# Reading q by feature, and a new order at the heads of the delta tiles, in a hybrid decoder layer on one core

## The reference: one layer of a hybrid decoder

```python
    qb = _l2norm(heads(qb, DK)) * (DK ** -0.5)      # x * rsqrt(sum(x * x) + eps)
    kb = _l2norm(heads(kb, DK))
...
def _gated_delta_chunk(S, q, k, v, g, beta):
    gc = jnp.cumsum(g, axis=-1)
    diff = gc[..., :, None] - gc[..., None, :]
    decay = jnp.where(incl, jnp.exp(jnp.where(incl, diff, 0.0)), 0.0)
    kk = jnp.einsum('bhid,bhjd->bhij', k, k)
    a_mat = jnp.where(strict, beta[..., :, None] * decay * kk, 0.0) + jnp.eye(L, dtype=jnp.float32)
    eg = jnp.exp(gc)
    rhs = beta[..., None] * (v - eg[..., None] * jnp.einsum('bhid,bhde->bhie', k, S))
    u = lax.linalg.triangular_solve(a_mat, rhs, left_side=True, lower=True, unit_diagonal=True)
    qk = jnp.einsum('bhid,bhjd->bhij', q, k) * decay
    o = eg[..., None] * jnp.einsum('bhid,bhde->bhie', q, S) + jnp.einsum('bhij,bhje->bhie', qk, u)
    S_new = jnp.exp(gc[..., -1])[..., None, None] * S + jnp.einsum('bhjd,bhj,bhje->bhde', k, w_last, u)
    return S_new, o
...
ob = _gated_rms_norm(ob, z, gdn_norm)               # o * rsqrt(mean(o * o) + eps) * w * silu(z)
gate = sigmoid(gate_logits); h = h + (ga * (oa @ w_oa) + gb * (ob @ w_ob)) @ w_out
```

## Time and profile before

| | us |
|---|---|
| median of three runs (lowest, highest) | 3335.37 (3330.85, 3346.25) |
| the profiled execution's own time | 3332.55 |
| its span | 3330.7 |
| TensorE busy, share of the span | 3247.1 (97%) |
| weight loads on TensorE, which overlap its products | 2841.8 (85%) |
| VectorE, ScalarE, GpSimd busy | 60%, 46%, 12% |

### The profile page before, as it was taken

One profiled execution on the slowest core, in us unless ns is written; L12 is line 12 of the kernel. 1 busy time (PEld: TensorE's weight loads), 2 busy tenths in 40 slices (PEclk: granted clock), 3 DMA queues, 4 the chain that ended last, 5 costly groups with the idle time before them and its releaser, 6 DMA issues. The chain is left out here.

```text
span 3330.7 us, 59185 instructions
## 1 busy us (share of the span) xinstructions
PE 3247.1 (97%) x23574; PEld 2841.8 (85%) x23574; DVE 1986.5 (60%) x3721; ACT 1520.0 (46%) x3173; POOL 413.5 (12%) x453
## 2 busy tenths in 40 slices
PE   8999899999999999999999999999999999999998
PEld 7877789999998777898998777889998777789896
DVE  6645545543547654685766754587575855578484
ACT  5324443222235554464554654455454654446362
POOL 2211100432503111000003011000001211000000
PEclk9989999999999999999999999999999999999999
DMA  4211013655743111354553211345463211246463
GB/s 161 63 56 46 25 58 111 229 194 199 257 154 110 54 46 63 116 160 138 165 193 109 73 39 46 114 137 167 137 213 124 78 44 43 80 129 183 124 177 97
DMA packets 142816, 392.47 MB, mean 118 GB/s; under 512 B 18288, under 2 KB 20288, under 8 KB 139072
## 3 DMA queue, kind: packets, MB, share of 16 engines
q1 hardware_dynamic: 142544, 388.69, 36.5%
HBM read 353.95 MB, written 35.69 MB: 117 GB/s over the span
## 5 line engine op out<-in xcount | busy, mean ns | idle before, releaser
L624 DVE TENSOR_TENSOR wl<-raw,wh 128x512 fp32r<-128x512 f32 (+1 forms) x795 | 747.1, 947 | 573.2 <-ACT wh L617 569.6
L617 ACT CAST wh<-raw 128x512 fp32r<-128x512 f32 (+1 forms) x795 | 636.0, 808 | 459.6 <-PE bank L892 370.8
L892 PE MATMUL bank<-xnT,wh 128*128 128x512 f32 (+2 forms) x2432 | 725.3, 382 | 9.0 <-ACT gate L1663 7.3
L892 PE MATMUL bank<-hnT,wh 128*128 128x256 f32 (+2 forms) x3016 | 580.7, 290 | 3.1 <-ACT V L1959 3.1
L892 PEld LDWEIGHTS bank<-xnT,wh 128*128 128x128 f32 x2432 | 430.3, 192 | 81.6 <-issue 16.5
L892 PEld LDWEIGHTS bank<-hnT,wh 128*128 128x128 f32 x3016 | 473.6, 188 | 8.5 <-ACT V L1959 3.7
L892 PE MATMUL bank<-hid,wh 128*128 128x512 f32 (+1 forms) x1760 | 467.6, 353 | 0.0
L892 PE MATMUL bank<-xnT,wl 128*128 128x512 f32 (+2 forms) x1280 | 461.8, 365 | 0.0
L892 PE MATMUL bank<-hnT,wl 128*128 128x256 f32 (+2 forms) x1508 | 437.2, 290 | 0.0
L892 PE MATMUL bank<-Tm,wh 128*128 128x256 f32 x2016 | 368.7, 282 | 0.2 <-ACT sg L1959 0.2
L892 PEld LDWEIGHTS bank<-hid,wh 128*128 128x128 f32 x1760 | 309.5, 188 | 46.0 <-issue 0.3
(11 more groups left out here) (380 smaller groups left out, 4527.3 us busy)
## 6 DMA issues: line engine op xcount, KB each, us to landing
raw<-in_wstream SPq DMA_DIRECT2D x346, 512.0 KB, 3.5
raw<-wsum SPq DMA_DIRECT2D x252, 256.0 KB, 3.4
raw<-in_wstream SPq DMA_DIRECT2D x189, 256.0 KB, 2.8
ops_in<-in_wstream SPq DMA_DIRECT2D x44, 512.0 KB, 7.6
wsum<-ops_out SPq DMA_DIRECT2D x22, 1024.0 KB, 6.3
hT<-in_xT SPq DMA_DIRECT2D x4, 2048.0 KB, 8.9
out_yp_out<-hT SPq DMA_DIRECT2D x16, 512.0 KB, 3.0
xr<-in_x_prompt SPq DMA_DIRECT2D x12, 512.0 KB, 7.9
```

The costliest lines, as they stand in the source:

```text
L617: act.copy(hi_cell(n), raw_cell(n)).then_inc(sem("hi_done"), 1)
L624: nc.vector.tensor_tensor(lo_cell(n), raw_cell(n), hi_cell(n).bitcast(F32), ALU.subtract).then_inc(sem("lo_done"), 1)
L892: ins = nc.tensor.matmul(*a, **k)
```

## The change

- The product of k and q (kq) reads q by feature straight from `post`, not normalised. Its norm factor is put on the output instead: GpSimd multiplies the sum of the output's squares by the square of the factor, and the root that it makes of it by the factor.
- `d_qn` and `d_qe` go, with their two transposes back and ScalarE's two copies of them. In their place ScalarE exponentiates the decay that TensorE has spread over a bank (`eG`, 128x512), and VectorE multiplies `post` by it (`scaled_q`, into `d_WQ`). The transpose of q to rows stays for tiles 1 to 3, whose sums of squares need it, and goes for the small tile and tile 0.
- VectorE at a tile's head: the arguments come right behind `d_kn`, the sum of q's squares (now three reductions, with the halves of two heads swapped) behind them; the weights' subtraction and `delta_out` come behind the masks, the scaled rows and `scaled_q`.
- ScalarE: the copy of the gate logits comes ahead of the cast of the next unit, which came first before. A unit that is done at k = 17 is cast at the next tile's head, behind the decays.
- Group 0's tables: in the small tile the state products go by head, with three quarters between them; tiles 0 to 2 get a quarter at k = 17; the last tile has seven in place of eleven. Of the small tile's own loop over the eight sequences (`S_FILL`) a quarter moves from b = 0 to b = 5.

```diff
-QUARTERS_S = (1, 1, 1, 1, 1, 1, 0, 0, 1, 0, 0, 0, 0, 1, 2, 6, 0, 0)
-QUARTERS_0 = (1, 1, 1, 0, 1, 1, 1, 1, 0, 1, 1, 0, 1, 0, 1, 0, 0, 0)
-S_FILL = (0, 3, 4, 6, 7, 8)
-assert sum(QUARTERS) * NT == 64 and QUARTERS_C + sum(QUARTERS_S) + sum(QUARTERS_0) * NT == 64
+QUARTERS_S = (1, 1, 1, 1, 1, 1, 0, 0, 1, 0, 0, 0, 0, 1, 3, 6, 0, 0)
+QUARTERS_0 = (1, 1, 1, 0, 1, 1, 1, 1, 0, 1, 1, 0, 1, 0, 1, 0, 0, 1)
+QUARTERS_E = (1, 0, 1, 0, 1, 0, 1, 0, 0, 1, 0, 0, 1, 0, 1, 0, 0, 0)
+S_FILL = (3, 4, 5, 6, 7, 8)
+assert sum(QUARTERS) * NT == 64 and QUARTERS_C + sum(QUARTERS_S) + sum(QUARTERS_0) * (NT - 1) + sum(QUARTERS_E) == 64
...
-        quarters_of = lambda t: QUARTERS_S if t == "S" else QUARTERS_0 if first else QUARTERS
+        quarters_of = lambda t: QUARTERS if not first else QUARTERS_S if t == "S" else QUARTERS_E if t == NT - 1 else QUARTERS_0
...
+                if q_rows(t):
+                    rows_from(t, 2, 0, "sqc_done", 2 * NH + 2 * t)
...
-                pe.wait_ge(*made("bt_rd", 3 * i + 2))
                 claim(2, "QK_done", i + 1)
                 for x in range(NH):
                     for cs in chunks(t):
-                        last = nc.tensor.matmul(bank[2][cs, w * x:w * (x + 1)], kTd[:, x, cs], qT[:, x, cs], start=True, stop=True)
+                        last = nc.tensor.matmul(bank[2][cs, w * x:w * (x + 1)], kTd[:, x, cs], q_of(x, cs), start=True, stop=True)
...
 
                 if first or t:
-                    turned(t, 0, 1, "kn")
-                    turned(t, 1, 3, "qn")
+                    turned(t)
                 beside(t, 0)
                 if first or t:
                     delta_scores(t)
-                if first or t:
-                    turned(t, 2, 5, "qe")
                     beside(t, 1)
...
                     for x in range(NH):
+                        if x:
+                            gate_quarter()
                         pair = WQ[:, x, 0:2 * CH].rearrange("p (s c) -> p s c", c=CH)
                         out = bank[3][:, 2 * CH * x:2 * CH * (x + 1)].rearrange("p (s c) -> p s c", c=CH)
                         for b in range(NB):
                             own = slice(NMETA + NL * b, NMETA + NL * (b + 1))
                             last = nc.tensor.matmul(out[:, :, own], Sb[:, b, x, :], pair[:, :, own], start=True, stop=True)
-                        if x == 1:
-                            gate_quarter()
                     last.then_inc(sem("WS_ps"), 1)
-                    gate_quarter()
...
-                hi_until("gate", j)
...
+                act.activation(eG[:, :, 0:n], bank[4][:, 0:NH * n].rearrange("p (h n) -> p h n", h=NH), ACT.Exp).then_inc(sem("dec_done"), 1)
...
                     if quarters[0] % 4 == 0:
                         gate_logits()
+                        if k != 17:
+                            gate_weights()
...
                 if first or t:
-                    turned_copy(t, 0, 1, "kTd")
-                    turned_copy(t, 1, 3, "qT")
-                    delta_decays(t)
+                    turned_copy(t)
+                    if t != 0:
+                        delta_decays(t)
+                    gate_weights()
                 beside(t, 0)
-                turned_copy(t, 2, 5, "qeT")
...
-                root(rr[0:n, 8:12], ss[0:n, 8:12], n, 1.0 / P, 4).then_inc(sem("orr_done"), 1)
+                own = lambda x: fac[0:n, slot(t), x, :]
+                link(nc.gpsimd.tensor_tensor(ss[0:n, 12:16], ss[0:n, 8:12], own(1), ALU.mult))
+                link(root(rr[0:n, 8:12], ss[0:n, 12:16], n, 1.0 / P, 4))
+                nc.gpsimd.tensor_tensor(rr[0:n, 8:12], rr[0:n, 8:12], own(0), ALU.mult).then_inc(sem("orr_done"), 1)
...
+            def scaled_q(t):
+
+                n = n_of(t)
+                dve.wait_ge(*made("dec_done", 10 * ix[t] + 6))
+                v_.tensor_tensor(WQ[:, :, CH:CH + n], post[:, 0:NH, col(t):col(t) + n], eG[:, :, 0:n], ALU.mult).then_inc(sem("natq_done"), 1)
+
+            def sum_k(t):
+
+                dve.wait_ge(*made("sqc_done", 2 * NH + 2 * t - 1))
+                v_.tensor_reduce(out=rs8[:, t + 1, NH:], in_=q4["kn"][:], op=ALU.add, axis=AX.X).then_inc(sem("sums_in"), 1)
+
+            def sum_q(t):
+
+                dve.wait_ge(*made("sqc_done", 2 * NH + 2 * t))
+                step(v_.tensor_reduce(out=rs8[:, t + 1, 0:2], in_=q4["qn"][:, 0:2], op=ALU.add, axis=AX.X))
+                for dst, src in HALVES:
+                    ins = v_.tensor_reduce(out=rs8[dst, t + 1, 2:NH], in_=q4["qn"][src, 2:], op=ALU.add, axis=AX.X)
+                    if dst.start == 0:
+                        step(ins)
...
-                if t == "S" or t and not first:
+                if t == "S":
                     delta_args(t)
-                if i:
-                    delta_out(tiles[i - 1])
                 beside(t, 0)
                 if first or t:
                     delta_masks(t)
-                    dve.wait_ge(*made("nat_ps", 3 * i + 3))
+                    dve.wait_ge(*made("nat_ps", nat_of(t, 2 + q_rows(t))))
+                    if q_rows(t):
+                        dve.wait_ge(*made("rs_done", 1 + F + 2 * t))
                     scaled(t, ("kb", "kw", "bv"))
+                    scaled_q(t)
+                    gate_weights()
                 else:
                     scaled(t, ("kb", "kw"))
                 beside(t, 1)
+                if i:
+                    delta_out(tiles[i - 1])
...
-                            row_sums_of(t + 1)
+                            sum_k(t + 1)
...
                             delta_rows(t + 1)
-                        if first and k == 1 and t + 1 < NT:
                             delta_args(t + 1)
+                            sum_q(t + 1)
                         beside(t, 15 + 2 * k)
```

More of the change, by code:

```diff
@@ L179 @@
         (0, 15, 12):
-            "bt_ps bt_rd nat_ps",
+            "",
         (0, 16, 0):
@@ L784, in group @@
         chunk_half = lambda x, k: k if x < NH // 2 else 1 - k
-        quarters_of = lambda t: QUARTERS_S if t == "S" else QUARTERS_0 if first else QUARTERS
+        quarters_of = lambda t: QUARTERS if not first else QUARTERS_S if t == "S" else QUARTERS_E if t == NT - 1 else QUARTERS_0
+        q_rows = lambda t: t not in ("S", 0)
+        nat_of = lambda t, k: sum(2 + q_rows(x) for x in tiles[:ix[t]]) + k
         def sync(sp):
@@ L1170, in delta_rows, with turned @@
                 last.then_inc(sem("G_ps"), 1)
-            def turned(t, q, b, src):
+            def turned(t):
                 i, n = ix[t], n_of(t)
-                pe.wait_ge(*made("natq_done", 6 * i + q + 1))
-                claim(b, "bt_rd", 3 * i + q + 1)
+                pe.wait_ge(*made("natq_done", 5 * i + 1))
+                claim(1, "bt_rd", i + 1)
                 for x in range(NH):
-                    last = nc.tensor.transpose(bank[b][:, n * x:n * (x + 1)], q4[src][0:n, x, :], c("ident")[0:n, 0:n])
+                    last = nc.tensor.transpose(bank[1][:, n * x:n * (x + 1)], q4["kn"][0:n, x, :], c("ident")[0:n, 0:n])
                 last.then_inc(sem("bt_ps"), 1)
@@ L1789, in scalar @@
                 gate_logits()
+                hi_until("gate", 0)
             def beside(t, k):
@@ L2367, in sums_copied @@
                 for n, sl in heads_of:
[L2368 removed]
+                    sums = bank[6][0:n, 8 * sl.start:8 * sl.stop].rearrange("p (t h) -> p t h", h=8)
+                    if n == P:
+                        step(v_.tensor_copy(rs8[:, sl, 0:2], sums[:, :, 0:2]))
+                        for dst, src in HALVES:
+                            step(v_.tensor_copy(rs8[dst, sl, 2:NH], sums[src, :, 2:NH]))
+                        v_.tensor_copy(rs8[:, sl, NH:], sums[:, :, NH:]).then_inc(sem("sums_in"), 1)
+                    else:
+                        v_.tensor_copy(rs8[0:n, sl, :], sums).then_inc(sem("sums_in"), 1)
+                settle()
             for j in range(NCONV):
@@ L2444, in beside @@
                     quarters[0] += 1
-                    if quarters[0] % 4 == 0:
-                        lo_until("gate", quarters[0] // 4 - 1)
+                    if quarters[0] % 4 == 0 and k != 17:
+                        gate_weights()
                     if first and quarters[0] % 4 == 2:
@@ L2450, in beside, with gate_weights @@
                     attention_step(after(t), IN_DELTA_S if t == "S" else IN_DELTA, k)
+            def gate_weights():
+                if quarters[0] >= 4:
+                    lo_until("gate", quarters[0] // 4 - 1)
             def delta_out(t):
```

99 lines of the change are left out of this document (51 added, 48 removed).

## The result

| | before | changed |
|---|---|---|
| median of 8 runs (lowest, highest), us | 3340.86 (3330.85, 3348.92) | 3354.72 (3349.59, 3357.66) |
| the profiled execution's own time | 3332.55 | 3352.43 |

The ratio is 1.0042, with a 95% interval of 1.0026 to 1.0058. The forecast was 3320, in a range of 3305 to 3335.

What follows compares the result with a forecast made beforehand. TensorE, busy for 97% of the span, was taken as the bound. Groups 1 to 3 (-2.2) and group 0 (-11.4) made -13.6, from 3332.55 to 3319 us; the forecast was 3320, range 3305 to 3335.

Steps and rivals of the forecast that it cites:

- Group 0: First group's tiles: transposes gone, waits filled and lower clock regained, less last tile and late cast: -11.4 us.
- Groups 1 to 3, tiles 1 and 2: Earlier head, mostly given back at `kT` by the late cast at k = 2: -0.1 us for each tile.
- 1.2 earlier at X's product: Tile head, groups 1 to 3: quarter starts 0.8 us earlier without `d_qn`, and `d_qe`'s transpose (0.41) goes.
- about 1.4: Tiles 1 and 2, groups 1 to 3: TensorE's wait for `kT` grows from 0.37 to about 1.4 us.
- Tile 3: Groups 1 to 3, no next tile's attention: casts ahead of X copies lose the head's gain and more, +0.15 us.
- Tile 0: Groups 1 to 3: two transposes back stay won (0.41 + 0.44), less 0.15 at `kT`: -0.7 us.
- The heads' waits: Group 0, tiles 1 to 3: a quarter of 1.39 us fills each 1.9 us wait for `d_kn`: -4.2 us.
- the wait of 2.2: Group 0 at 335, ahead of the exponentials: goes as units end at k = 2, 7 and 14: -2.2 us.
- the lower clock at 297 and 335: Group 0's slow stretches, with others 10 us in all; somewhat over half regained: -5.5 us, bounds -10 and 0.
- The last tile: Group 0: four quarters given up (5.6 us), mostly uncovered, +3.5 us, and +1.7 for one lower-clock stretch.
- The wait at `kT` drops the clock: Rival, chance 0.10, slower: `kT` waits in 12 tiles each cost 1.7 us of lower clock: 3345 us.
- The first rival: Chance 0.33: `kT` is not late and all lower clock in group 0 goes: 3308 us.

Runs made afterwards that it cites:

- cast-first version: Changed kernel, but ScalarE casts the next unit's weights ahead of the gate copy inside a tile (k = 17 still postponed): 3300.84 us, 0.9892; repeated 3310.30 us, 0.9914.

## Why the prediction was wrong, point by point

**The sum.** From the end of one tile to that of the next, groups 1 to 3 were to change by -0.7, -0.1, -0.1 and +0.15 us in tiles 0 to 3. In group 1 it was +1.85 (from the transposes of tile 0's rows on), +0.91, +0.98 and +1.60: 5.3 a group in place of -0.75, some 16 in all. Group 0, which was to give 11.4, lost 3. So of the 33 us between forecast and profiled run somewhat over half lie in groups 1 to 3.

**What failed.** The step "Groups 1 to 3, tiles 1 and 2": I wrote that "two casts that now share ScalarE with the attention's exponentials can cost 0.1 more". It was 1.19 us a tile (1.12 of wait), in the nine tiles of groups 1 to 3 that have a next one, because I followed the cast at k = 6 on ScalarE alone. VectorE's subtraction waits for it, and `pTm` stands behind that. The order of VectorE at the head was in the document; that at k = 6, where the same pair of instructions stands, I did not lay out. The run with the subtraction behind the attention shows the cause; the one with the late cast in the kernel before shows that nothing else of the change is needed.

**Head and `kT`.** "1.2 earlier at X's product" was 1.14, and "about 1.4" at `kT` was 1.25 in tiles 1 and 2. Both right. The run with the cast ahead at k = 17 confirms the 0.8 for the gate copy as 0.7. That VectorE would come to the masks in time was right too.

**Tile 3.** "+0.15" was 1.6 us. The late cast at k = 2 raised the wait for X's copy from 0.62 to 1.56, and some 1.6 us of lower clock followed in each group. Mis-sized, and its second half is the mechanism that I had as a rival for `kT`.

**Tile 0.** "-0.7" was +1.85. The wait at L1120 is there again (1.13). The two transposes back are gone as I had it, and the wait for `kT` did not grow at all (0.80 before, 0.82 now). But the scores wait once more behind it, for the bank that `d_bv` frees:

```profile
1130.24 1.13 PE L1094 MATMUL bank<-kT,qTt 64*128 64x256 f32 x6 [0.71 <-DVE d_bv L2295]
```

```profile
1127.89 1.69 DVE L628 TENSOR_TENSOR wl<-raw,wh 128x1024 fp32r<-128x1024 f32 x1 [1.93 <-ACT wh L621]
1129.51 0.68 DVE L2295 TENSOR_TENSOR d_bv<-bank,beta 128x512 f32<-128x512 f32 x1
```

It is the step that failed at k = 6, at k = 2: the subtraction waits for the late cast, and `d_bv` stands behind it. And the bank's wait ahead of the gate's transposes, which I let absorb q's rows, did more than that: 0.44 became 1.41, while the rows that are gone took 0.43. VectorE, which frees that bank, now (1103.03 to 1103.76) copies the sums of squares in four parts ahead of it in place of one.

**Group 0.** -11.4 was predicted; the changed kernel is 3.0 us behind at group 1's first kk product. The heads' waits, the wait of 2.2, the lower clock at 297 and 335 and all but one of the gate copy's waits ahead of quarters went as I had them. The kernel was 8.2 ahead at tile 0, and lost that lead behind it, by three things.

- A unit that now ends at k = 14 put cast and subtraction ahead of the state's update: 1.64 us at L1392 in each of tiles 0 to 2 and 2.2 in the last, with lower clock behind the second one (342 to 346). No term had it. With the cast ahead of the copy that wait is gone.
- The new tables put the unit's end ahead of products of the attention that wait for the small gate copy: six waits of 0.48 at L1120 and L1128 in tiles 0 to 2. The run of the kernel before with the new tables has them as well. No term had them either.
- The last tile was mis-sized. The prediction lets the quarters' own time come off the place that they leave, so the tile was to change by -5.6 + 3.5 + 1.7 = -0.4. It took 9.3 more, from its kk product to the second block behind the tiles. Before, and with the change:

```profile
410.60:457.85 47.25, 43.57 (x463) 35.79 (x463) 18.18 (x43) 19.11 (x58) 5.19 (x7) 0.96 0.11 35
```

```profile
406.09:462.68 56.59, 46.79 (x419) 38.08 (x420) 17.86 (x44) 17.36 (x53) 9.48 (x17) 0.70 0.06 20
```

TensorE is idle for 9.8 us in place of 3.7, and most of the rest is the clock, 0.70 in place of 0.96.

**The rivals.** "The wait at `kT` drops the clock" was named as the slower case. The profiled run of the changed kernel has no lower clock behind `kT`; it has it behind X. But other kernels with the cast late at k = 2 have it. With the cast ahead everywhere but at k = 2, these 4 us follow tile 0's waits for `kT` and `d_bv` (0.82 and 0.72) in group 1:

```profile
1120.00:1124.00 4.00, 4.00 (x24) 2.73 (x24) 2.53 (x14) 0.00 (x0) 0.00 (x0) 0.50 0.27 102
```

Five kernels have that cast late, with fifteen such tiles 0 in groups 1 to 3; five of these tiles take 1.5 to 3.1 us longer than the others of their kernel, all with a lower clock there, and none of the 24 in the other profiled runs does. So what this rival names does happen, in some tiles of some executions, and is the smaller cost. The sign came from a wait that I had not seen (L1120, with the subtraction ahead of `d_bv`), from group 0, and from the clock at other places than I had feared. The first rival's 3308 is near the cast-first version (3301 and 3310), in which `kT` is in time and the clock mostly kept; that is a kernel with another order on ScalarE, and no point for the rival.

**The clock.** The Trainium skill ("TensorE: Matmul & The Clock Gate", section "A second HAM failure mode: psum-queue depth-cycling") has, for a bf16 kernel, brief idle times between groups of products as a cause of a swinging clock. The traces agree with it for group 0's last tile and for 1279 to 1287, and they limit it: the cast-first version has waits of up to 1.9 us in a last tile with the same quarters, and in one of its profiled runs it keeps 1.00 there, in the other 0.89.

## What to carry to other kernels

When an instruction is moved on one engine, follow each engine that waits for its result, and on each look at what stands behind the waiting one. Here a cast that cost nothing where it was cost a microsecond twice per tile one place later, once in its own queue and once in that of the engine that consumes it. If a step has a producer and a consumer on two in-order engines, look at both places: the change had moved the consumer at the tile's head, and there it was right, and moving it at k = 6 too took that wait away, but not the one in ScalarE's own queue. And a filler taken from a stage with waits can cost more than its own time if the clock falls behind it: the changed kernel's last tile took 9.3 us more with 5.6 us less work, while with the casts in front the same table lost nothing.

## What the runs showed of the hardware that was not expected

- The eight runs of the changed kernel line up with their mean granted clock: 3349.59 us at 0.989, 3351.03 and 3352.43 at 0.988, 3354.70, 3354.74 and 3356.15 at 0.987, 3357.40 and 3357.66 at 0.986. As an estimate from these, 0.003 of 3350 us are 10 us of full clock, and the runs spread over 8.1: the spread is about that of the time at the lower clock.
- The lower clock comes without idle time too: the small tile's stretch without the split has TensorE busy for 16.00 of 16 us and a clock of 0.52.
- Stretches of lower clock differ between executions of the same code: the cast-first version's last tile has 1.00 in one profiled run and 0.89 in the other, which follows, and the small tile has 1.00 in both, but 0.59 in the run that is the same program up to there:

```profile
196.00:212.00 16.00, 15.33 (x116) 13.74 (x116) 1.15 (x3) 1.53 (x5) 0.00 (x0) 1.00 0.11 34
398.00:444.00 46.00, 39.19 (x418) 31.88 (x414) 17.46 (x42) 17.53 (x54) 9.48 (x17) 0.89 0.08 26
```

What decides between the two is open; no run here tells it.
